# Where TensorE does the attention's small steps: head sums, a first exchange and the last scores moved into the midst of projections

## The chip, the cores and the metric

The kernel runs on one core of one Trainium2 chip. The metric is the device time of one execution in microseconds. Three runs of the kernel before gave 2029.91, 2032.22 and 2032.23 us, a median of 2032.22.

## The reference

A trunk of four layers over 256 tokens of width 1024, all in fp32. Each layer is a feed-forward block, a mixer and a feed-forward block:

```python
for i in range(DEPTH):                       # DEPTH = 4
    x = x + 0.5 * _swiglu(_rms_norm(x, norm_ffn1[i]), ...)
    h = _rms_norm(x, norm_mix[i])
    y = fox (i = 0, 3), conv module (i = 1), diff attention (i = 2)
    x = x + y
    x = x + 0.5 * _swiglu(_rms_norm(x, norm_ffn2[i]), ...)
```

The change touches the two kinds of attention. Fox has 16 heads of 64; q and k are RMS-normalised per head, and a cumulated forget gate is added to the scores before a causal softmax:

```python
q = _rms_norm(q, q_gain); k = _rms_norm(k, k_gain)
s = einsum(q, k) * scale + cum_q - cum_k     # cum: running sum of log_sigmoid(forget logits)
p = softmax(where(causal, s, -inf));  o = einsum(p, v);  y = o @ w_out
```

Diff attention has 8 heads of twice 64; q and k get a partial rotary embedding after the norm, and two softmaxes are combined:

```python
q = _partial_rope(_rms_norm(q, q_gain), cos, sin); k likewise
a = p[:, :, 0] - lam * p[:, :, 1];  o = _rms_norm(einsum(a, v), sub_gain) * (1 - lambda_init)
y = o @ w_out
```

## The kernel before

The activations stay transposed in SBUF, 8 tiles of 128 features by 256 tokens. Every weight is read once, in blocks of 1 MB: a DMA puts a block into one of five raw slots, ScalarE (ACT) rounds it to its high part (`split_high`, line 468), VectorE (DVE) subtracts to get the low part (`split_low`, line 774), and TensorE (PE) multiplies in three passes, high by high, low by high and high by low (lines 1332 to 1334). In the attention each such pass has 256 moving columns.

Each engine has its own program, an order written out by hand; an engine works strictly in that order and waits on semaphores that the others raise. There is no planner. So the place of a call in an engine's list decides what waits behind it.

An attention phase has four groups of 256 features (4 heads in fox, 2 double heads in diff). For group j PE does the projections of q (bank 0), k (bank 1) and v (bank 2), each block in two halves of 24 matmuls, and between them the small steps for group j and for the attention of group g = j - 1:

- `head_sums("q")`, `head_sums("k")` (line 1585): the squares of q or k, made by ACT (line 575), are summed over each head by a matmul with a matrix of ones. ACT takes Ln and Exp of the result (lines 567, 570, tiles q_inv, k_inv), and DVE multiplies (`normed`, line 992). In fox both sums go into bank 3, and k's waits until ACT has read q's (`q_log_ready`). k's products give kT, from which the scores of the next step are made.
- `swapped` (line 1590, diff): PE exchanges the rotated features by a permutation matrix; DVE multiplies by sines and cosines (lines 1001, 1007) and adds (line 1014).
- `score_pair(r)` (line 1531, in fox also 1539 for the gates): scores of two heads into banks 4 and 5. DVE masks and takes the maximum (lines 1025 or 1028, and 1032), ACT exponentiates (line 582), DVE normalises (line 1044) or combines (`combine`, lines 1055 and 1060).
- `turn(m)` (line 1552) transposes the probabilities, ACT copies them out (line 602, tile probsT), and `values(m)` (lines 1569, 1570) multiplies them with v. The second fox `score_pair` waits until the copies 0 and 1 are made, for it writes over their banks.

After the last group comes a tail: the attention of group 3 stands among the four blocks of the output projection, `o_block` (48 matmuls each, for o_part of groups 0 to 3). In diff, `o_sums` (line 1595) makes the norm of o.

The lists of ACT and DVE matter as much. In diff, for j of 2 and 3, ACT does in this order: o_squares, split_high(b+3j+2), inverse("o"), square("q"), o_part, exps(0), inverse("q"), exps(1), split_high(b+3j+3), copy_probs(0), square("k"), split_high(b+3j+4), exps(2), exps(3), inverse("k"), copy_probs(1). DVE does: split_low(b+3j+2), o_normalised, raw_part("q"), mask 0 and 1, o_part, normed("q"), combine(0), split_low(b+3j+3), rotary_cos("q"), raw_part("k"), mask 2, rotary_sin("q"), mask 3, rotary_sum("q"), split_low(b+3j+4), combine(1), normed("k"), and the rotary steps of k. In fox, for j of 1 to 3, ACT ends with exps(2), square("k"), inverse("q"), exps(3), split_high(b+3j+4), inverse("k"), copy_probs(2), copy_probs(3).

In fox's group 0 DVE also splits the cumulated gates (`split_cum`), and then GpSimd (POOL) spreads them over the heads in four instructions (`spread_cums`, line 424), while DVE goes on.

Of the kernel before, what the change touches and what calls it, by code (L numbers as in the profile page):

```python
# [18 lines left out]
KT = D // P  # L19
# [39 lines left out]
def build_trunk(nc, A, out):  # L59
# [12 lines left out]
    with ExitStack() as ctx:  # L72
# [106 lines left out]
        u = u_pad[:, :, TAPS - 1:TAPS - 1 + SEQ]  # L179
# [7 lines left out]
        bank = [banks[:, i, :] for i in range(8)]  # L187
# [271 lines left out]
        def _(act):  # L459
# [97 lines left out]
            def attention(i):  # L557
                a, b, fox = number(i), starts[i], phases[i] == "fox"
# [60 lines left out]
                def fox_group(j, u=0):  # L619

                    g = j - 1
                    split_high(b + 3 * j + 2)
                    if not j:
                        softplus()
                    square("q", j, u)
                    if j:
                        exps(0, g, u)
                        exps(1, g, u)
                    split_high(b + 3 * j + 3)
                    if j:  # L630
                        copy_probs(0, g, u)
                        copy_probs(1, g, u)
                        exps(2, g, u)
                    square("k", j, u)
                    inverse("q", j, u)
                    if j:
                        exps(3, g, u)
                    split_high(b + 3 * j + 4)
                    inverse("k", j, u)
                    if j:  # L640
                        copy_probs(2, g, u)
                        copy_probs(3, g, u)
                        o_part(g, u)
# [125 lines left out]
        def _(dve):  # L769
# [202 lines left out]
            def attention(i):  # L972
# [152 lines left out]
                def fox_group(j, u=0):  # L1125
                    g = j - 1
                    if not j:
                        logits()
                    split_low(b + 3 * j + 2)
                    if not j:  # L1130
                        cumulate()
                    raw_part("q", j, u)
                    if j:
                        mask_and_max(0, g, u)
                        mask_and_max(1, g, u)
                        normalise(0, g, u)
                        normalise(1, g, u)
                        split_low(b + 3 * j + 3)
                        mask_and_max(2, g, u)
                        raw_part("k", j, u)  # L1140
                        mask_and_max(3, g, u)
                    else:
                        raw_part("k", j, u)
                        split_low(b + 3 * j + 3)
                        split_cum()
                    normed("q", j, u)
                    if j:
                        normalise(2, g, u)
                        normalise(3, g, u)
                    split_low(b + 3 * j + 4)  # L1150
                    normed("k", j, u)
                    values(j, u)
                    if j:
                        o_part(g, u)
# [175 lines left out]
        def _(pe):  # L1330
# [178 lines left out]
            def attention(i):  # L1509
# [88 lines left out]
                def fox_group(j, u=0):  # L1598
                    g = j - 1
                    q_blk, k_blk, v_blk = (b + 3 * j + n for n in range(3))  # L1600
                    if j:
                        wait_block(q_blk)
                        columns_half(bank[0], q_blk, 0)
                        columns_half(bank[0], q_blk, 1).then_inc(S["block_done"], 1)
                        score_pair(0, g, u)
                    else:
                        first_block(i, bank[0])
                        forget_gates()
                    wait_block(k_blk)
                    columns_half(bank[1], k_blk, 0)  # L1610
                    columns_half(bank[1], k_blk, 1).then_inc(S["block_done"], 1)
                    if j:
                        turn(0, g, u)
                        turn(1, g, u)
                    else:
                        turn_cum()
                    head_sums("q", j, u)
                    wait_block(v_blk)
                    if j:
                        pe.wait_ge(S["v_ready"], 4 * a + j + u)  # L1620
                    tokens_half(bank[2], v_blk, 0, range(3))
                    if j:
                        score_pair(1, g, u)
                    tokens_half(bank[2], v_blk, 0, range(3, KT))
                    if j:
                        values(0, g, u)
                        values(1, g, u)
                    head_sums("k", j, u)
                    tokens_half(bank[2], v_blk, 1, range(6))
                    if j:  # L1630
                        turn(2, g, u)
                        turn(3, g, u)
                    tokens_half(bank[2], v_blk, 1, range(6, KT)).then_inc(S["block_done"], 1)
                    if j:
                        values(2, g, u)
                        values(3, g, u)

                def diff_group(j, u=0):
                    g = j - 1
                    q_blk, k_blk, v_blk = (b + 3 * j + n for n in range(3))  # L1640
                    if j:
                        wait_block(q_blk)
                        columns_half(bank[0], q_blk, 0)
                        if j > 1:
                            o_sums(g - 1, u)
                        columns_half(bank[0], q_blk, 1).then_inc(S["block_done"], 1)
                        score_pair(0, g, u)
                        head_sums("q", j, u)
                    else:
                        first_block(i, bank[0])  # L1650
                    wait_block(k_blk)
                    columns_half(bank[1], k_blk, 0)
                    columns_half(bank[1], k_blk, 1).then_inc(S["block_done"], 1)
                    if j:
                        turn(0, g, u)
                        score_pair(1, g, u)
                        swapped("q", j, u)
                    else:
                        head_sums("q", j, u)
                    wait_block(v_blk)  # L1660
                    if j:
                        pe.wait_ge(S["v_ready"], 4 * a + j + u)
                    tokens_half(bank[2], v_blk, 0)
                    if j:
                        values(0, g, u)
                    head_sums("k", j, u)
                    if not j:
                        swapped("q", j, u)
                    tokens_half(bank[2], v_blk, 1).then_inc(S["block_done"], 1)
                    if j:  # L1670
                        turn(1, g, u)
                    swapped("k", j, u)
                    if j:
                        values(1, g, u)

                def forget_gates():
# [23 lines left out]
                if fox:  # L1700
                    fox_group(0)
                    for j in range(1, GROUPS):
                        fox_group(j)
                    score_pair(0, g, 0)

                    pe.wait_ge(S["v_ready"], 4 * a + GROUPS)
                    o_block(0)
                    turn(0, g, 0)
                    turn(1, g, 0)
                    score_pair(1, g, 0)  # L1710
                    o_block(1)
                    values(0, g, 0)
                    values(1, g, 0)
                    turn(2, g, 0)
                    turn(3, g, 0)
                    o_block(2, (0, 4))
                    values(2, g, 0)
                    values(3, g, 0)
                    o_block(2, (4, KT))
                    o_block(3)  # L1720
                else:
                    for j in range(GROUPS):
                        diff_group(j)
                    score_pair(0, g, 0)
                    o_sums(g - 1, 0)

                    pe.wait_ge(S["v_ready"], 4 * a + GROUPS)
                    o_block(0)
                    turn(0, g, 0)
                    score_pair(1, g, 0)  # L1730
                    o_block(1, (0, 4))
                    values(0, g, 0)
                    o_block(1, (4, KT))
                    turn(1, g, 0)
                    o_block(2, (0, 1))
                    values(1, g, 0)
                    o_block(2, (1, 4))
                    o_sums(g, 0)
                    o_block(2, (4, KT))
                    o_block(3)  # L1740

            def conv(i):
# [82 lines left out]
```

## Time and profile before

| | |
|---|---|
| runs | 2029.91, 2032.22, 2032.23 us |
| profiled execution | 2030.45 us, span from first to last instruction 2028.7 us |
| mean granted TensorE clock | 0.999 |
| PE busy | 1984.2 us, 98% of the span |
| DVE busy, ACT busy | 1424.9 us (70%), 1046.1 us (52%) |
| first fox phase, diff phase, second fox phase | about 207 to 342, 1196 to 1334, 1702 to 1837 us |

The profile page gives such busy times, the chain that ended last and the costliest groups of instructions. The queries behind it give the instructions of a stretch in order of time, with the idle time of the engine ahead of each and what ended it, and sums of waits. A busy time of 98% is a share of the whole span; what the change can do is decided in the places where PE stands idle in the three attention phases.

### The profile page before, as it was taken

How to read it: one execution, taken by the hardware profiler on the slowest of the kernel's cores; microseconds unless marked ns; L12 is line 12 of the kernel's file. 1: busy time of each engine (PE TensorE's matmuls, PEld its weight loads, DVE VectorE, ACT ScalarE, POOL GpSimd, SP SyncE). 2: the span in 40 equal slices, each digit the busy share in tenths (PEclk: the TensorE clock that was granted, in tenths of full speed). 3: DMA queues.
4: the chain of work that ended last, by engine and by line, in shares of the span. 5: the costliest groups of instructions: out<-in, count | busy, mean ns of one | idle time of the engine just before them, and what ended most of it. 6: DMA issues, size and time to landing. Idle time of an engine off the chain costs nothing.

```text
span 2028.7 us, 29076 instructions
## 1 busy us (share of the span) xinstructions
PE 1984.2 (98%) x12584; PEld 1742.9 (86%) x12584; DVE 1424.9 (70%) x1631; ACT 1046.1 (52%) x1247; POOL 110.2 (5%) x120
## 2 busy tenths in 40 slices
PE   7999999999999998999999999999999999999999
PEld 6888888888888896988888888888888888888887
DVE  6876767876787554777587658887658765778763
ACT  5644456654555344654365455665446545456542
POOL 1000201000200001100000000010010001101000
PEclk9999999999999999999999999999999999999999
DMA  6655433655665583565656553355565555335653
GB/s 209 201 187 183 146 125 113 200 189 184 188 188 186 185 247 88 183 191 182 193 187 193 175 182 125 110 182 187 177 197 187 187 183 172 125 114 177 187 182 108
DMA packets 336365, 350.14 MB, mean 173 GB/s; under 512 B 10077, under 2 KB 331886, under 8 KB 336238
## 3 DMA queue, kind: packets, MB, share of 16 engines
q1 hardware_dynamic: 331742, 343.58, 53.3%
q10 hardware_dynamic: 4496, 4.70, 1.0%
q8 instruction: 99, 1.62, 0.3%
q14 instruction: 28, 0.23, 0.0%
HBM read 346.04 MB, written 2.22 MB: 172 GB/s over the span
## 4 chain that ended last, share of the span: by engine, by line
PE 89%; DVE 5%; ACT 4%; issue 1%; DMA 1%; ACTq 0%; SPq 0%; DVEq 0%
PE banks L1341 48%; PE banks L1346 25%; PE banks L1332 4%; PE banks L1333 4%; PE banks L1334 4%; ACT sb_w_high L468 1%; DVE sb_w_low L774 1%; ACT sb_scores L582 1%; PE banks L1531 1%; PE banks L1761 1%; PE banks L1569 1%; DMA sb_raw<-in_ffn_w_up 1%; DVE sb_neg_max L1032 0%; PE banks L1585 0%; PE banks L1552 0%
## 5 line engine op out<-in xcount | busy, mean ns | idle before, releaser
L774 DVE TENSOR_TENSOR sb_w_low<-sb_raw,sb_w_high 128x2048 fp32r<-128x2048 f32 (+1 forms) x332 | 752.4, 2271 | 241.3 <-ACT sb_w_high L468 240.9
L1341 PE MATMUL banks<-sb_x_both,sb_w_high 128*128 128x512 f32 x2816 | 727.0, 394 | 7.1 <-DVE sb_x_both L818 7.1
L468 ACT ACTIVATE sb_w_high<-sb_raw 128x2048 fp32r<-128x2048 f32 (+1 forms) x332 | 618.7, 1867 | 155.9 <-DMA sb_raw<-in_ffn_w_down 113.7
L1341 PEld LDWEIGHTS banks<-sb_x_both,sb_w_high 128*128 128x128 f32 x2816 | 500.9, 189 | 89.8 <-issue 7.5
L1346 PEld LDWEIGHTS banks<-sb_x_both,sb_w_low 128*128 128x128 f32 x2816 | 398.3, 190 | 36.0
L1346 PE MATMUL banks<-sb_x_both,sb_w_low 128*128 128x256 f32 x2816 | 408.1, 282 | 0.0
L1341 PE MATMUL banks<-sb_h_both,sb_w_high 128*128 128x512 f32 x1408 | 360.7, 395 | 0.0
L1341 PEld LDWEIGHTS banks<-sb_h_both,sb_w_high 128*128 128x128 f32 x1408 | 251.6, 188 | 46.7
L1346 PEld LDWEIGHTS banks<-sb_h_both,sb_w_low 128*128 128x128 f32 x1408 | 194.6, 188 | 17.1
L1346 PE MATMUL banks<-sb_h_both,sb_w_low 128*128 128x256 f32 x1408 | 200.3, 282 | 0.0
L1332 PE MATMUL banks<-sb_x_both,sb_w_high 128*128 128x256 f32 x512 | 148.7, 291 | 0.0
L486 ACT ACTIVATE sb_x_both<-sb_xT,sb_vec 128x256 fp32r<-128x256 f32 x96 | 43.6, 502 | 197.9 <-DVE sb_xT L807 176.7
L1333 PE MATMUL banks<-sb_x_both,sb_w_high 128*128 128x256 f32 x512 | 144.8, 283 | 0.0
L1334 PE MATMUL banks<-sb_x_both,sb_w_low 128*128 128x256 f32 x512 | 144.8, 283 | 0.0
L527 ACT ACTIVATE sb_up_part<-banks 128x512 f32<-128x512 f32 x88 | 52.4, 596 | 178.6 <-PE banks L1341 178.6
L527 ACT ACTIVATE sb_gate_part<-banks 128x512 f32<-128x512 f32 x88 | 52.4, 596 | 165.5 <-PE banks L1341 165.5
L931 DVE TENSOR_TENSOR sb_up_part<-banks,sb_up_part 128x512 f32<-128x512 f32 x88 | 60.7, 689 | 63.7 <-ACT sb_up_part L527 63.7
L1332 PEld LDWEIGHTS banks<-sb_x_both,sb_w_high 128*128 128x128 f32 x512 | 98.1, 192 | 3.2 <-issue 3.0
L1333 PEld LDWEIGHTS banks<-sb_x_both,sb_w_high 128*128 128x128 f32 x512 | 98.1, 192 | 1.6 <-issue 1.4
L915 DVE TENSOR_TENSOR sb_gate_part<-banks,sb_gate_part 128x512 f32<-128x512 f32 x88 | 60.7, 690 | 54.6 <-ACT sb_gate_part L527 54.4
L1334 PEld LDWEIGHTS banks<-sb_x_both,sb_w_low 128*128 128x128 f32 x512 | 98.1, 192 | 0.0
L804 DVE SCALAR_TENSOR_TENSOR sb_xT<-banks,sb_xT 128x512 f32<-128x512 f32 x32 | 22.1, 691 | 98.6 <-PE banks L1341 98.6
(210 smaller groups left out, 1950.8 us busy)
## 6 DMA issues: line engine op xcount, KB each, us to landing
sb_raw<-in_ffn_w_gate SPq DMA_DIRECT2D x88, 1024.0 KB, 5.4
sb_raw<-in_ffn_w_up SPq DMA_DIRECT2D x88, 1024.0 KB, 5.4
sb_raw<-in_ffn_w_down SPq DMA_DIRECT2D x64, 1024.0 KB, 5.0
sb_raw<-in_ffn_w_down SPq DMA_DIRECT2D x32, 768.0 KB, 4.3
sb_raw<-in_fox_w_in SPq DMA_DIRECT2D x24, 1024.0 KB, 5.2
sb_raw<-in_conv_w_pw SPq DMA_DIRECT2D x12, 1024.0 KB, 5.4
sb_raw<-in_diff_w_in SPq DMA_DIRECT2D x12, 1024.0 KB, 5.1
sb_raw<-in_fox_w_out SPq DMA_DIRECT2D x8, 1024.0 KB, 4.9
```

What stands on the lines that cost most here:

```text
L468: act.activation(slot(w_high, b)[:, 0:width(b)], slot(raw, b)[:, 0:width(b)], ACT.Copy).then_inc(S["high_ready"], 1)
L486: act.activation(x_high[:, t, :], xT[:, t, :], ACT.Copy, scale=vec[:, col + t:col + t + 1]).then_inc(S["xhigh_ready"], 1)
L527: act.activation((up_part if which else gate_part)[:, :, :], banks[:, at:at + 2, SEQ:], ACT.Copy).then_inc(S["up_part_ready" if which else ...
L774: dve.tensor_tensor(slot(w_low, b)[:, 0:width(b)], slot(raw, b)[:, 0:width(b)], slot(w_high, b)[:, 0:width(b)].bitcast(F32), ALU.subtract) ...
L804: dve.scalar_tensor_tensor(xT[:, 2 * T:2 * T + 2, :], sums[:, :, SEQ:], 0.5, xT[:, 2 * T:2 * T + 2, :], ALU.mult, ALU.add).then_inc(S["x_h ...
L915: dve.tensor_tensor(gate_part[:, :, :], banks[:, at:at + 2, 0:SEQ], gate_part[:, :, :], ALU.add).then_inc(S["gate_sum_ready"], 1)
L931: dve.tensor_tensor(up_part[:, :, :], banks[:, at:at + 2, 0:SEQ], up_part[:, :, :], ALU.add).then_inc(S["up_sum_ready"], 1)
L1332: pe.matmul(dst, s_high, m_high, start=first, stop=False, skip_group_check=loose)
L1333: pe.matmul(dst, s_high, m_low, start=False, stop=False, skip_group_check=loose)
L1334: return pe.matmul(dst, s_low, m_high, start=False, stop=last, skip_group_check=loose)
L1341: return pe.matmul(pair(bank[at][:, :]), high[:, n * P:(n + 1) * P], m_both, start=first, stop=last, skip_group_check=True)
L1346: pe.matmul(bank[at][:, SEQ:2 * SEQ], low[:, n * P:(n + 1) * P], m_high, start=False, stop=False, skip_group_check=True)
```

## The change

Only orders are changed; no instruction is added or removed, and every operand, semaphore and bank stays. Some calls are cut in two ranges. Fox:

- Group 0: ACT and DVE split block b+4 after inverse("k") and normed("k"), not ahead of them.
- Groups 1 to 3: PE's `head_sums("k")` comes after the first 3 of 8 tiles (9 matmuls) of v's second half, not ahead of them.
- Tail: 3 of 8 column tiles (18 matmuls) of `o_block(1)` come ahead of `score_pair(1)`.

Diff:

- Group 0's `swapped("k")` goes from the end of group 0 to the middle of group 1's q block.
- Groups 1 to 3: `head_sums("q")` goes from ahead of the k block to the middle of it (24 matmuls later).
- Tail: half of `o_block(0)` (24 matmuls) comes ahead of `score_pair(0)`, and `o_sums(3)` comes one column tile (6 matmuls) earlier within `o_block(2)`.

```diff
 # ACT, fox_group (DVE's fox_group likewise, with split_low and normed)
-                    split_high(b + 3 * j + 4)
+                    if j:
+                        split_high(b + 3 * j + 4)
                     inverse("k", j, u)
+                    if not j:
+                        split_high(b + 4)
 # PE, fox_group
-                    head_sums("k", j, u)
-                    tokens_half(bank[2], v_blk, 1, range(6))
+                    else:
+                        head_sums("k", j, u)
+                    tokens_half(bank[2], v_blk, 1, range(3))
+                    if j:
+                        head_sums("k", j, u)
+                    tokens_half(bank[2], v_blk, 1, range(3, 6))
 # PE, diff_group
                         if j > 1:
                             o_sums(g - 1, u)
+                        else:
+                            swapped("k", 0, u)
                         columns_half(bank[0], q_blk, 1).then_inc(S["block_done"], 1)
                         score_pair(0, g, u)
-                        head_sums("q", j, u)
...
                     columns_half(bank[1], k_blk, 0)
+                    if j:
+                        head_sums("q", j, u)
                     columns_half(bank[1], k_blk, 1).then_inc(S["block_done"], 1)
...
-                    swapped("k", j, u)
-                    if j:
+                    if j:
+                        swapped("k", j, u)
                         values(1, g, u)
 # PE, tail of fox
+                    o_block(1, (0, 3))
                     score_pair(1, g, 0)
-                    o_block(1)
+                    o_block(1, (3, KT))
 # PE, tail of diff
+                    o_block(0, (0, 4))
                     score_pair(0, g, 0)
                     o_sums(g - 1, 0)
-                    o_block(0)
+                    o_block(0, (4, KT))
...
-                    o_block(2, (1, 4))
+                    o_block(2, (1, 3))
                     o_sums(g, 0)
-                    o_block(2, (4, KT))
+                    o_block(2, (3, KT))
```

## Rows read from the trace of the kernel before

**Rows 1.** The page: PE's busy time, its share of the span, instructions.
```profile
PE 1984.2 (98%) x12584; PEld 1742.9 (86%) x12584; DVE 1424.9 (70%) x1631; ACT 1046.1 (52%) x1247; POOL 110.2 (5%) x120
```
**Rows 2.** Sums of PE's waits: total us, times, longest us.
```profile
PE banks L1585 <- ACT sb_q_inv L567: 4.8, 6, 0.8
```
**Rows 3.** PE in time order, third fox group: start, us, instruction, idle ahead.
```profile
279.94 1.10 PE L1585 MATMUL banks<-sb_k_square,sb_ones_heads 128*128 128x512 f32 x2 [0.80 <-ACT sb_q_inv L567]
...
284.80 0.81 PE L1569 MATMUL banks<-sb_probsT,sb_v_nat 128*64 128x256 f32 x3 [0.25 <-ACT sb_probsT L602]
```
**Rows 4.** ACT in time order, the same group.
```profile
277.71 0.40 ACT L582 ACTIVATE sb_scores<-sb_scores,sb_neg_max 128x128 f32<-128x128 f32 x1 [3.80 <-DVE sb_neg_max L1032]
...
281.24 1.90 ACT L468 ACTIVATE sb_w_high<-sb_raw 128x2048 fp32r<-128x2048 f32 x1
...
284.28 0.85 ACT L602 ACTIVATE sb_probsT<-banks 128x384 f32<-128x384 f32 x2
```
**Rows 5.** DVE in time order, fox, end of group 0.
```profile
231.44 3.98 DVE L774 TENSOR_TENSOR sb_w_low<-sb_raw,sb_w_high 128x2048 fp32r<-128x2048 f32 x1
235.34 2.38 DVE L992 SCALAR_TENSOR_TENSOR sb_kT<-sb_gate_scaled,sb_vec,sb_k_inv 128x512 f32<-128x512 f32 x1
...
238.43 3.19 DVE L774 TENSOR_TENSOR sb_w_low<-sb_raw,sb_w_high 128x2048 fp32r<-128x2048 f32 x1
```
**Rows 6.** POOL in time order, the same stretch (four instructions merged).
```profile
229.08 10.40 POOL L424 TENSOR_TENSOR sb_wide<-sb_cum_parts,sb_head_of_row 128x1024 bf16<-128x1024 bf16 x4 [17.18 <-DVE sb_cum_parts L1116]
```
**Rows 7.** PE in time order, fox group 1: first scores, second turn.
```profile
237.82 0.93 PE L1531 MATMUL banks<-sb_kT,sb_qT 64*128 64x128 f32 x8 [0.92 <-issue]
...
246.41 0.55 PE L1552 MATMUL banks<-sb_ident,sb_scores 128*128 128x128 f32 x3 [0.60 <-DVE sb_scores L1044]
```
**Rows 8.** PE in time order, fox tail: second scores, third and fourth turn.
```profile
321.09 0.93 PE L1531 MATMUL banks<-sb_kT,sb_qT 64*128 64x128 f32 x8 [0.72 <-ACT sb_probsT L602]
...
328.94 0.88 PE L1552 MATMUL banks<-sb_ident,sb_scores 128*128 128x128 f32 x6
```
**Rows 9.** DVE in time order, fox tail: the last normalisation.
```profile
326.01 0.55 DVE L1044 TENSOR_SCALAR sb_scores<-sb_scores,sb_inv_sum 128x128 f32<-128x128 f32 x2
```
**Rows 10.** PE in time order, diff: exchange of group 0, q's head sum of group 1.
```profile
1218.52 1.13 PE L1590 MATMUL banks<-sb_gate_scaled,sb_swap 128*128 128x512 f32 x2 [1.31 <-DVE sb_gate_scaled L992]
...
1227.09 1.13 PE L1585 MATMUL banks<-sb_q_square,sb_ones_heads 128*128 128x512 f32 x2 [0.85 <-ACT sb_q_square L575]
```
**Rows 11.** PE in time order, diff group 2, and group 3's first scores.
```profile
1251.72 0.28 PE L1333 MATMUL banks<-sb_x_both,sb_w_high 128*128 128x256 f32 x1
1251.84 0.28 PE L1334 MATMUL banks<-sb_x_both,sb_w_low 128*128 128x256 f32 x1
1252.05 0.93 PE L1531 MATMUL banks<-sb_kT,sb_qT 64*128 64x128 f32 x8
1253.57 1.12 PE L1585 MATMUL banks<-sb_q_square,sb_ones_heads 128*128 128x512 f32 x2 [0.59 <-ACT sb_q_square L575]
...
1278.78 0.93 PE L1531 MATMUL banks<-sb_kT,sb_qT 64*128 64x128 f32 x8
```
**Rows 12.** ACT in time order, diff group 2: Ln of q's head sums.
```profile
1255.08 0.67 ACT L567 ACTIVATE sb_q_inv<-banks,sb_eps 128x512 f32<-128x512 f32 x1
```
**Rows 13.** DVE in time order, diff group 2.
```profile
1259.13 2.29 DVE L774 TENSOR_TENSOR sb_w_low<-sb_raw,sb_w_high 128x2048 fp32r<-128x2048 f32 x1 [0.20 <-ACT sb_w_high L468]
...
1269.68 0.74 DVE L992 SCALAR_TENSOR_TENSOR sb_gate_scaled<-sb_gate_scaled,sb_vec,sb_k_inv 128x512 f32<-128x512 f32 x1
```
**Rows 14.** PE in time order, diff tail: first scores, first turn.
```profile
1300.01 0.93 PE L1531 MATMUL banks<-sb_kT,sb_qT 64*128 64x128 f32 x8 [1.02 <-DVE sb_kT L1014]
...
1308.22 0.55 PE L1552 MATMUL banks<-sb_ident,sb_scores 128*128 128x128 f32 x3 [0.48 <-DVE sb_scores L1060]
```
**Rows 15.** Stretches at the conv phase's idle: length; PE, PEld, DVE, ACT, POOL busy; PEclk; DMA.
```profile
795.40:800.40 5.00, 0.00 (x0) 0.00 (x0) 4.42 (x6) 3.69 (x6) 0.00 (x0) 1.00 0.00 0
800.40:803.80 3.40, 2.83 (x13) 2.83 (x14) 1.49 (x3) 3.34 (x7) 0.00 (x0) 0.51 0.00 0
```

More of the change, by code:

```diff
@@ L1149, in fox_group @@
                         normalise(3, g, u)
-                    split_low(b + 3 * j + 4)
+                    if j:
+                        split_low(b + 3 * j + 4)
                     normed("k", j, u)
+                    if not j:
+                        split_low(b + 4)
                     values(j, u)
```

## Prediction

> **What bounds the kernel now.** The page comes first: PE is busy 98% of the span [rows 1], so anything gained must come from the places where it idles. The sums of waits name them: the largest that this change aims at is PE at a head sum, waiting for ACT's reading of bank 3, six times 0.8 us [rows 2]. But a wait tells only where PE stands, not what sets the time. So I read next PE, ACT and DVE in time order through one group of each phase, and asked of each wait: if PE didn't wait here, would it wait at its next meeting with the same chain? The reader is to see in rows 3 and 4, and in 11 to 13, that ACT and DVE run without a gap from one meeting with PE to the next. There PE's idle time is only slack of a loop whose length the other two engines set. Single projection matmuls start 0.12 us apart [rows 11]; 24 of them take 2.9 us, a full block 5.8.
>
> **Fox, groups 1 to 3: 0.** The head sum of k waits 0.80 [rows 3]. Put 9 matmuls (1.1 us) later it needs no wait, so PE is some 0.7 us early at turn(2). The next meeting is values(2), which already waits 0.25 for ACT's copies [rows 3]. ACT's list there is exps(2) at 277.71 (after 3.80 of idling for the mask, that is for PE's second scores), squares, both halves of q's inverse, exps(3), split_high at 281.24, k's inverse, copies at 284.28, with no gap from 277.71 on [rows 4]. k's inverse runs behind split_high (281.24 + 1.90 = 283.1); the head sum, now at about 280.3, is done by 281.4. So the copies come when they did, values(2) starts at 284.80 as before, and its wait grows from 0.25 to about 1. Six waits of 0.8 go and six of 0.7 to 0.8 come. What would be lost without that cover is nothing either: one more switch between kinds of matmul costs PE about 0.1, inside the new wait.
>
> **Fox, group 0: +0.1 a phase.** PE waits 0.92 for the first scores [rows 7], for kT is made at 235.34, behind split_low(b+4), which starts at 231.44 [rows 5]. With the order turned, DVE makes kT first. But DVE is slow here because POOL works: kT takes 2.38 where the same line takes 0.74 in diff, and w_low 3.98 and 3.19 where it takes 2.29 there [rows 5, 13], while POOL's four instructions stretch over 10.40 us [rows 6]. Taking turns, with POOL first: kT runs 231.44 to 233.9, w_low of b+4 233.8 to 237.9, v 237.8 to 238.6, w_low of b+5 238.6 to 241.8, where it ended at 241.62 before. So the scores start at 236.9, 0.9 early; block b+4 is ready at 237.9, just when PE comes (236.9 + 1.1). The next meeting is turn(1), which waits 0.60 for DVE's normalisation [rows 7], and DVE does that behind the second w_low and the masks, without a gap. It moves by +0.1. Bounds: 0 if the order costs DVE nothing, +1.9 if DVE loses one turn more to POOL (10.40 / 4 = 2.6 with waiting, less 0.7 of waiting); I take the row nearest, the unchanged total.
> The Trainium skill, "SBUF — State Buffer", section "SBUF: two separate sides", says that VectorE and GpSimd take a shared pair of ports by an exclusive lock for a whole instruction. The trace agrees (2.38 against 0.74), and by that rule the turns come out as above; were it bandwidth that is shared, kT would end a little earlier, with the same sum.
>
> **Fox, tail: -0.8 a phase.** The second scores wait 0.72 for both copies [rows 8]. Now 18 matmuls (2.2 us, and 0.1 for a switch) stand there, and the scores start at 322.4, not 321.09: +1.35. Everything behind them on DVE and ACT is 1.35 later: the last normalisation ends at 326.01 + 0.55 + 1.35 = 327.9. PE, with the wait gone, reaches turn(2) at 328.94 - 0.8 = 328.1 [rows 8, 9]. It just fits, 0.2 to spare and 0.3 more for turn(3). The copies and the last o_low have over 1 us of cover (24 more matmuls of o_block(2)). Bounds: -0.4 if turn(3) waits, -0.8. I take -0.8.
>
> **Diff, group 1: +0.35.** `swapped("k")` of group 0 waits 1.31 [rows 10]. In the middle of the q block it doesn't: q's first half begins at 1217.1, the exchange stands at 1220.0, DVE reads it at 1221.3 as before, and the first scores start at 1223.85 and not at 1227.09 - 0.85 - 0.93 = 1225.3: 1.45 early. But the head sum of q now comes 24 matmuls behind them: 1223.85 + 0.93 + 2.9 = 1227.7, against 1227.09. ACT read it 3.03 after the first scores before (as in rows 11 and 12: 1255.08 - 1252.05), at 1228.35; now ACT can have it 1.05 behind its start (its record, whose end is modelled, is 1.12 long [rows 11]), at 1228.7. So q's inverse comes 0.35 later, and with it all below.
>
> **Diff, groups 2 and 3: +1.85 each. This is the step that decides.** Before, the head sum of q waits 0.59 for ACT's squares (1253.57, which is 1.52 behind the scores at 1252.05) [rows 11]; ACT takes its Ln at 1255.08, straight behind exps(0) [rows 12]. After, PE does 24 matmuls first: 1252.05 + 0.93 + 2.9 = 1255.9 for the head sum, and 1.05 more for ACT, 1256.95. Waiting in ACT's queue behind q's inverse are exps(1) and split_high(b+3j+3); DVE's normed("q"), combine(0) and split_low(b+3j+3) wait for those (the last by 0.20 at 1259.13) [rows 13], and DVE then has no idle moment until k's norm at 1269.68 [rows 13]. PE starts the next group's first scores 9.10 behind that (1278.78) [rows 11], by its own work and one more exchange. So the loop is: scores to k's norm 17.63, set by ACT and DVE; k's norm to scores 9.10, set by PE; together 26.73. The first part grows by 1256.95 - 1255.08 = 1.85 (1.8 to 1.95). PE's own work in that part has fewer waits than before and isn't the limit: the first turn waits about 1.2, the second about 1.4. Bounds: -0.7 a group (PE's wait of 0.59 and its switch saved, if PE's list alone set the time), +1.85. The value next to the rows is the upper, for they show no gap.
>
> **Diff, tail: +1.7.** The first scores wait 1.02 for kT; 24 matmuls ahead of them take 2.9 with a switch: +1.8 net. Scores to first turn is 8.21, at whose end PE already waits 0.48 for DVE's combine [rows 14]; this part isn't shortened, and now only 24 matmuls lie in it, so PE idles some 3.4 us there. The earlier o_sums(3) finds its squares not quite ready and gains 0.1.
>
> **Sum.** Fox 2 x (0 + 0.13 - 0.8) = -1.3; diff 0.35 + 2 x 1.85 + 1.7 = +5.75; together +4.4 us. DMA has no part: no attention split waits for a landing, and the loads, released by block_done, move by under 2 us at most. On the profiled execution (2030.45) that makes 2034.9; it lies 1.8 under the median of the three runs, whose two upper ones agree within 0.01. I give 2036.2, near the median plus 4.4 (2036.6), a bit toward the profiled one.
>
> **Rivals.**
> 1. *The waits simply go.* Head sums 6 x 0.8; first scores of fox 2 x 0.92; second scores of the tails 2 x 0.72; diff 1.31, 0.85, 2 x 0.59, 1.02: 12.4 us, less 0.8 for the switches: 2020.6. For it: each of these waits is truly there. Against it: values(2) and the turns wait already.
> 2. *Diff's chain has slack after all; the kernel is not slower.* If q's norm isn't what split_low(b+3j+3) hangs on, groups 2 and 3 are PE's: -0.7 each, group 1 -1.45, tail +1.7, fox -1.3: -2.4, so 2029.8. It decides at ACT's Ln of q: it must not come later than exps(0) ends. For it: PE's wait at the second turn is under 0.2. Against it: 24 matmuls are 2.9 us, the slack there 0.5.
> 3. *The clock falls in the new idle time of diff's tail.* After the conv phase's idle of 5 us the granted clock was 0.51 (1.2 and not 2.4 GHz) for 3.4 us, in which PE made 13 matmuls in 2.83 us, 0.1 us more for each: 1.3 us [rows 15]. In the tail it would add up to that: 2037.5. Against it: 3.4 us is shorter than 5. The Trainium skill, "TensorE: Matmul & The Clock Gate", section "HAM oscillation — how this bites in real kernels", warns of such gaps; by that rule the time would be this 2037.5; the trace agrees for the idle of 5 us [rows 15].
> 4. *DVE loses a turn to POOL in fox's group 0.* +1.9 in each fox phase: 2039.8. Block b+4 would come late, and turn(1) too.
>
> **Chances.** Forecast 0.67, rival 1 0.05, rival 2 0.13, rival 3 0.08, rival 4 0.07. Range: 2031.5 to 2039.0; it leaves out rival 1, half of rival 4 and most of rival 2. Two medians of this kernel are told apart at about 0.2%, that is 4.1 us, and the forecast lies hard by it: of its chance I put 0.4 to slower and 0.27 to the same; rivals 3 and 4 are nearly all slower (0.13), rival 1 faster (0.05); of rival 2 0.03 is faster and 0.10 the same. Faster 0.08, same 0.39, slower 0.53.
>
> **What would show it.** Right: in groups 2 and 3 of diff first scores to first scores takes 28.6 and not 26.7, ACT waits for PE at q's Ln, and PE waits over 1 us at both turns; in fox the wait of the k head sum is gone, values(2) waits about 1 us, and the group still takes 26.4; diff's tail has an idle of about 3.4 at the first turn; fox's tail is 0.8 shorter. Wrong: a diff group of 26 us, or a fox group under 26. In that case the chain that I call closed has a gap which I didn't see.

## The result: 0.4% slower, more than forecast

The changed kernel took 2040.48 us, the median of five runs (2036.3 to 2042.7), and the kernel before 2032.22 beside it. The ratio is 1.0042 (95% interval 1.0031 to 1.0052), +8.3 us where the forecast's sum had +4.4. The forecast was 2036.2 and its range ended at 2039.0, so the time lies above it. The same kernel measured again on another occasion gave 2037.74 beside 2031.02, a ratio of 1.0033 (1.002 to 1.0046); that is inside the range, but not for the forecast's reasons, as is shown below.

The profiled execution took 2042.7 us, with a span of 2040.9, 12.2 us longer than that of before. Page, busy times (answers to [rows 1]):

```profile
PE 1991.9 (98%) x12584; PEld 1747.8 (86%) x12584; DVE 1424.0 (70%) x1631; ACT 1046.0 (51%) x1247; POOL 110.1 (5%) x120
```

PE has the same 12584 matmuls and is 7.7 us longer busy: part of the loss is inside the matmuls and not in waits. The sums of PE's waits, as in [rows 2] (total us, times, longest), first before, then changed:

```profile
PE banks L1552 <- DVE sb_scores L1044: 1.9, 4, 0.6
...
PE banks L1569 <- ACT sb_probsT L602: 1.5, 6, 0.3
...
PE banks L1552 <- DVE sb_scores L1060: 0.5, 1, 0.5
```
```profile
PE banks L1558 <- DVE sb_scores L1063: 10.1, 7, 3.4
...
PE banks L1575 <- ACT sb_probsT L602: 5.5, 6, 0.9
PE banks L1558 <- DVE sb_scores L1047: 3.8, 4, 1.3
```

The head sums of k no longer wait: the 4.8 us of [rows 2] are gone. In their place `values` waits for ACT's copies 5.5 us where it waited 1.5, the turns of diff wait for DVE's combine 10.1 where it was 0.5, and those of fox for its normalisation 3.8 where it was 1.9. Nearly every wait went to PE's next meeting with the same chain; only the 0.72 ahead of the second scores in each fox tail [rows 8] did not come back.

PE in diff, in time order (start, us, instruction, idle ahead), answers to [rows 11, 14]: first scores of groups 1 to 3 and of the tail, head sums of q, turns of group 2, and the tail's first turn.

```profile
1226.82 0.93 PE L1537 MATMUL banks<-sb_kT,sb_qT 64*128 64x128 f32 x8
...
1255.41 0.93 PE L1537 MATMUL banks<-sb_kT,sb_qT 64*128 64x128 f32 x8
1259.24 1.02 PE L1591 MATMUL banks<-sb_q_square,sb_ones_heads 128*128 128x512 f32 x2
...
1264.22 0.55 PE L1558 MATMUL banks<-sb_ident,sb_scores 128*128 128x128 f32 x3 [1.10 <-DVE sb_scores L1063]
...
1275.06 0.55 PE L1558 MATMUL banks<-sb_ident,sb_scores 128*128 128x128 f32 x3 [1.12 <-DVE sb_scores L1063]
...
1284.01 0.93 PE L1537 MATMUL banks<-sb_kT,sb_qT 64*128 64x128 f32 x8
...
1308.89 0.93 PE L1537 MATMUL banks<-sb_kT,sb_qT 64*128 64x128 f32 x8
...
1317.13 0.90 PE L1558 MATMUL banks<-sb_ident,sb_scores 128*128 128x128 f32 x3 [3.39 <-DVE sb_scores L1063]
```

First scores to first scores: 28.59 and 28.60 us, where [rows 11] have 26.73. ACT in group 2 (as [rows 12]) and DVE's norm of k (as [rows 13]):

```profile
1260.30 0.69 ACT L567 ACTIVATE sb_q_inv<-banks,sb_eps 128x512 f32<-128x512 f32 x1 [1.76 <-PE banks L1591]
```
```profile
1274.92 0.75 DVE L995 SCALAR_TENSOR_TENSOR sb_gate_scaled<-sb_gate_scaled,sb_vec,sb_k_inv 128x512 f32<-128x512 f32 x1
```

ACT, which had no gap there, now waits 1.76 for PE's head sum. It takes q's Ln 4.89 behind the scores, 1.86 later than before. Scores to k's norm is 19.51 (17.63 before), and k's norm to the next scores 9.09 (9.10 before).

Granted clock by stretches of the same execution (length; PE, PEld, DVE, ACT, POOL busy with counts; PEclk; DMA share; GB/s):

```profile
1310.00:1316.20 6.20, 3.74 (x26) 3.06 (x25) 4.19 (x15) 5.14 (x12) 0.00 (x0) 1.00 0.19 49
1316.20:1323.03 6.83, 5.90 (x27) 4.92 (x28) 5.50 (x14) 2.94 (x11) 0.00 (x0) 0.50 0.32 111
1323.03:1330.00 6.97, 6.97 (x57) 6.79 (x56) 3.73 (x7) 3.54 (x3) 0.00 (x0) 1.00 0.12 24
776.90:780.30 3.40, 3.40 (x40) 2.16 (x36) 3.40 (x3) 3.38 (x5) 0.00 (x0) 0.50 0.19 40
800.80:807.60 6.80, 4.11 (x19) 4.11 (x20) 4.00 (x7) 6.51 (x12) 0.00 (x0) 0.50 0.01 2
1753.10:1756.50 3.40, 3.40 (x15) 2.62 (x15) 2.29 (x1) 0.93 (x3) 0.00 (x0) 0.51 0.39 139
```

In the midst of the new idle time of diff's tail the clock went to its lower level (PEclk 0.50, that is 1.2 GHz), and came back at 1323.0. Its 27 matmuls would take about half of their 5.90 us at the full clock (an estimate). The next two stretches stand in the conv phase, which the change doesn't touch, and the last in group 1 of the second fox phase.

Where the time went, by the starts of the same matmuls before and after, in us against the kernel before:

| stretch | orders, forecast | this profile | second profile of the same kernel |
|---|---|---|---|
| before the first fox phase | 0 | +0.15 | -0.43 |
| first fox phase | -0.67 | -0.81 | +0.75, with one stretch at half clock |
| conv phase | 0 | +3.73 | -1.27 |
| diff phase | +5.75 | +8.41, with one stretch at half clock | +5.80, none |
| second fox phase | -0.67 | +0.72, with one stretch at half clock | -0.79, none |
| whole span | +4.4 | +12.2 | +4.1 |

### The profile page after: what moved, and what is told of

It reads as the page before. It is cut to its first block, busy times and chain, and to the rows that moved or that the text cites. A ratio compares the mean times of both kernels' runs of the same rounds, so it can differ in the third digit from the quotient of the medians.

```text
span 2040.9 us, 29079 instructions
## 1 busy us (share of the span) xinstructions
PE 1991.9 (98%) x12584; PEld 1747.8 (86%) x12584; DVE 1424.0 (70%) x1631; ACT 1046.0 (51%) x1247; POOL 110.1 (5%) x120
## 4 chain that ended last, share of the span: by engine, by line
PE 90%; DVE 4%; ACT 4%; issue 1%; DMA 1%; ACTq 0%; SPq 0%; DVEq 0%
PE banks L1347 48%; PE banks L1352 25%; PE banks L1338 4%; PE banks L1339 4%; PE banks L1340 4%; ACT sb_w_high L468 1%; DVE sb_w_low L777 1%; ACT sb_scores L582 1%; PE banks L1537 1%; PE banks L1776 1%; DMA sb_raw<-in_ffn_w_up 0%; PE banks L1591 0%; PE banks L1575 0%; DVE sb_neg_max L1035 0%; DMA u_away<-sb_u_pad 0%
```

## The experiments

Theory O: what counts is how late the chain of ACT and DVE is fed, so each part has the price that the forecast gave it by orders alone. Theory C: beside it the gathered idle times let the clock fall, and that is the rest. Rival W: the waits that were removed are worth what they show. The kernel before had a median of 2031.02 beside the first four kernels of the table, 2031.17 beside the next four and 2031.12 beside the last four; differences below are between medians.

| kernel | what it has of the change | median, us (runs) | ratio, 95% |
|---|---|---|---|
| fox_parts | all of fox | 2029.98 (11) | 0.9998 (0.9989 to 1.0006) |
| diff_groups | diff's groups | 2034.74 (11) | 1.0020 (1.0011 to 1.0029) |
| diff_tail | diff's tail | 2034.74 (11) | 1.0021 (1.0012 to 1.0030) |
| after_again | all | 2037.74 (5) | 1.0033 (1.0020 to 1.0046) |
| diff_tail_filled | diff's tail, idle time filled | 2032.91 (11) | 1.0010 (1.0001 to 1.0019) |
| good_parts | fox groups 1 to 3 and tail, `swapped("k")`, `o_sums(3)` | 2029.91 (11) | 0.9996 (0.9987 to 1.0005) |
| fox_split_early | below | 2022.74 (5) | 0.9957 (0.9945 to 0.9969) |
| both_improved | below | 2020.58 (5) | 0.9944 (0.9932 to 0.9957) |
| f0_alone | order in fox's group 0 | 2031.78 (11) | 1.0005 (0.9996 to 1.0013) |
| q_sum_6 | head sum of q after 6 matmuls | 2031.51 (11) | 1.0002 (0.9993 to 1.0011) |
| q_sum_24 | head sum of q after 24 | 2037.14 (7) | 1.0032 (1.0020 to 1.0043) |
| after_tail_back | all but the tail's scores | 2034.01 (11) | 1.0016 (1.0007 to 1.0025) |

**The parts: fox_parts, diff_groups, diff_tail, after_again.** The first three have one phase's part of the diff each, the fourth is the changed kernel itself.

> Only the fox parts of the change (order of the splits in group 0, the later head sum of k, 18 matmuls ahead of the second scores in the tail). Theory 'orders and clock': the orders give -0.8 us in each fox tail and +0.1 in each group 0, -1.3 together, but the waits of PE in fox's group 1, which now stand together at the first and second turn (1.4 + 0.6 us), let the clock fall in some runs, about +1.4 each time: 2031 to 2033. In the profile a fox group takes 26.4 us as before and values(2) waits about 1 us. Rival 'the orders alone': no loss by the clock, -1.3 in every run: 2031. Rival 'the waits simply go': -8 us, 2024.

> Only two parts: swapped('k') of diff's group 0 in the middle of group 1's q block, and the head sum of q in the middle of the k block. Theory 'orders and clock': +0.3 in group 1, +1.85 in each of groups 2 and 3, +4.0 together, and the tail as before: 2036.2 if the clock stays up. First scores to first scores 28.6 us. Rival 'the change's loss of 8 us is all order, the diff groups are mis-sized': +6 or more here, with a longer group than 28.6.

> Only the two parts in diff's tail: half of o_block(0) ahead of the first scores, o_sums(3) one column tile earlier. Theory 'orders and clock': +1.7 by the order (first scores to first turn stays 8.2 us, PE idles 3.7 us in it), and after that idle the clock falls to half for 3.4 or 6.8 us, which costs 1.3 to 2.7 more: 2035 to 2036.6. Rival 'the orders alone': the fall of the clock in the changed kernel was chance, here it stays up: 2033.9.

> The changed kernel once more, for its clock and for the conv phase. Theory 'orders and clock': +4.3 us by the orders, the rest by stretches at half clock: each profile shows the same intervals between PE's steps where the clock is up, and the low stretches differ in number from one run to the next; 2036 to 2043. If the conv phase's loss of 3.7 us in the first profile is chance, it is gone here or seen in the other kernels too; if it belongs to the change, it is here again and in none of the three others.

diff_groups: the diff phase +4.05 in its profile, no half clock in it; the forecast's 0.35 + 2 x 1.85 exactly. diff_tail: the diff phase +3.29, of which the order is 1.8 (the phase is +1.77 in the filled kernel below) and the rest the clock. fox_parts: each phase gives back its 0.8 and then loses 1.55 at half clock, where 0.7 of gain stood in the orders. So in these profiles O holds for the sizes of the orders in every part, and C for what is beside them. The medians of the three parts, -1.0, +3.7 and +3.7, add up to +6.4, beside +6.7 for the whole. fox_parts can't be told from the kernel before, and it came out 1.0 us under the range that was expected for it: its profile, with a fall of the clock in both phases, is one of its slower runs. diff_groups came out 1.5 under its 2036.2, which was counted from the first occasion's median for the kernel before. Fox in the profile of fox_parts, group 1: PE in time order, and two stretches by clock.

```profile
244.72 0.55 PE L1558 MATMUL banks<-sb_ident,sb_scores 128*128 128x128 f32 x3 [1.32 <-DVE sb_scores L1047]
245.86 0.55 PE L1558 MATMUL banks<-sb_ident,sb_scores 128*128 128x128 f32 x3 [0.60 <-DVE sb_scores L1047]
246.24 1.72 PE L1591 MATMUL banks<-sb_q_square,sb_ones_heads 128*128 128x512 f32 x2
```
```profile
243.50:246.40 2.90, 1.08 (x7) 0.85 (x8) 1.84 (x8) 2.72 (x7) 0.00 (x0) 1.00 0.59 164
246.40:249.80 3.40, 3.40 (x12) 2.21 (x10) 2.29 (x1) 1.18 (x3) 0.00 (x0) 0.51 0.48 168
```

Before, the waits of this place lay apart: 0.92 at the first scores, 0.60 at the second turn [rows 7], and at the first turn this one:

```profile
245.27 0.55 PE L1552 MATMUL banks<-sb_ident,sb_scores 128*128 128x128 f32 x3 [0.35 <-DVE sb_scores L1044]
```

With kT made earlier the 0.92 is gone, and its time stands at the first turn (1.32, not 0.35), close to the 0.60. Behind those two the clock is at 1.2 GHz, and the head sum takes 1.72 instead of 1.02.

**The idle time in diff's tail: diff_tail_filled.** It is diff_tail with 24 matmuls on a free bank, whose results nobody reads:

```diff
                     o_block(0, (4, KT))
+                    for _ in range(24):
+                        pe.matmul(bank[7][:, 0:SEQ], x_high[:, 0, 0:P], x_high[:, 0, :], start=True, stop=True)
                     turn(0, g, 0)
```

> The kernel of diff_tail with 24 more matmuls (2.9 us, of activations that are at hand, into bank 7, whose old content has been read and which values(0) overwrites later) ahead of the first turn, where PE idles 3.7 us. Theory 'the clock falls through the idle': the matmuls cost nothing, since they lie in the idle; the order's +1.7 stays (first scores to first turn 8.2 us), but no stretch at half clock follows, so +1.7 over the kernel before instead of diff_tail's +3.7. Rival 'the half clock has nothing to do with this idle': it is seen behind the tail here too, and the time is diff_tail's.

PE at scores and first turn and the stretches by clock, first diff_tail, then filled:

```profile
1303.11 0.93 PE L1531 MATMUL banks<-sb_kT,sb_qT 64*128 64x128 f32 x8
...
1311.35 0.55 PE L1552 MATMUL banks<-sb_ident,sb_scores 128*128 128x128 f32 x3 [3.39 <-DVE sb_scores L1060]
1311.82 1.45 PE L1531 MATMUL banks<-sb_kT,sb_qT 64*128 64x128 f32 x8
```
```profile
1312.10:1315.50 3.40, 3.40 (x19) 2.75 (x17) 3.40 (x9) 1.24 (x5) 0.00 (x0) 0.50 0.13 44
```
```profile
1302.86 0.93 PE L1531 MATMUL banks<-sb_kT,sb_qT 64*128 64x128 f32 x8
...
1307.54 3.04 PE L1731 MATMUL banks<-sb_x_both 128*128 128x256 f32 x24
1311.10 0.55 PE L1552 MATMUL banks<-sb_ident,sb_scores 128*128 128x128 f32 x3 [0.51 <-DVE sb_scores L1060]
1311.57 0.93 PE L1531 MATMUL banks<-sb_kT,sb_qT 64*128 64x128 f32 x8
```
```profile
1312.10:1315.50 3.40, 3.40 (x29) 3.07 (x26) 3.39 (x10) 1.18 (x6) 0.00 (x0) 1.00 0.05 16
```

Scores to first turn is 8.24 in both, so the chain takes what it took and the extra matmuls cost nothing. But behind the turn the same 3.40 us hold 29 records instead of 19, and the second scores take 0.93 instead of 1.45. The median falls from +3.7 to +1.7, which is the order's own price. The two were run on different occasions and the intervals of their ratios just overlap (1.0012 to 1.0030 and 1.0001 to 1.0019), but 10 of diff_tail's 11 runs took 2034.0 or more, and 9 of the filled kernel's 11 took 2033.6 or less. So filling the idle time took the fall away: that the idle time let the clock fall is shown as far as one profile of each and the medians can show it. W is out here: with useless work in place of the wait the kernel is faster.

**How late may q's head sum be: q_sum_6, q_sum_24.** Both are the kernel before with only this call moved within the k block.

```diff
                         score_pair(0, g, u)
-                        head_sums("q", j, u)
...
-                    columns_half(bank[1], k_blk, 0)
+                    columns_half(bank[1], k_blk, 0, range(2))     # q_sum_6; q_sum_24: the whole half
+                    if j:
+                        head_sums("q", j, u)
+                    columns_half(bank[1], k_blk, 0, range(2, KT))
```

> Only q's head sum of diff's groups 1 to 3, put 6 matmuls (0.7 us) into the k block instead of ahead of it. Theory 'a closed chain of ACT and DVE': PE's wait of 0.59 us there goes, ACT's Ln of q comes when it did (behind exps(0), 0.5 us later than it could), and the time is that of the kernel before within 0.5 us; the saved wait comes back at the turns. Rival 'PE's waits are the time': -0.6 in each of three groups, -1.8.

> Only q's head sum of diff's groups 1 to 3, put 24 matmuls (2.9 us) into the k block as in the change; the exchange of group 0 stays where it was. Theory 'a closed chain': +1.85 in each of three groups, for group 1's first scores no longer come 1.5 us early: +5.5 by the order, 2036.7. If the exchange in the q block had no part in it, it would be +4.0 as in diff_groups.

ACT's Ln of q in group 2, first with 6 matmuls ahead, then with 24:

```profile
1255.34 0.67 ACT L567 ACTIVATE sb_q_inv<-banks,sb_eps 128x512 f32<-128x512 f32 x1
```
```profile
1259.88 0.69 ACT L567 ACTIVATE sb_q_inv<-banks,sb_eps 128x512 f32<-128x512 f32 x1 [1.76 <-PE banks L1585]
```

With 6 the wait of 0.59 [rows 11] is gone, ACT's Ln still comes straight behind its exponentials, and the kernel is as fast as before (+0.4, unclear against 0). A group takes 26.72. Of PE's 2.0 us of waits at these head sums 1.4 stand again at the turns. With 24 ACT waits 1.76, a group takes 28.61, and the kernel loses 6.0 us, three times 1.85 and a little (5.6 in the diff phase of its profile). The wait was worth nothing, the lateness all.

**The clock falls behind other gathered waits, and one order costs nothing: good_parts, f0_alone, after_tail_back.** They are made of parts of the diff alone; the last is the changed kernel with the first scores of diff's tail where they were.

> The change without its three parts that I hold to be harmful: left out are the order of the splits in fox's group 0, q's head sum in the midst of the k block, and o_block(0) ahead of the first scores. Theory: -0.8 in each fox tail, 0 from the later head sum of k, 0 or +0.1 from the exchange in the q block (S to k's norm is then ACT's and DVE's), -0.1 from o_sums(3): -1.6, with no stretch at half clock in any attention phase: 2029.4. If the fall of the clock in fox's group 1 has nothing to do with where PE's waits stand, it is seen here as well, at about 246 or 1741 us.

> Only the order of the splits in fox's group 0 (block b+4 behind k's norm). Theory 'waits gathered in one place let the clock fall': by the order +0.1 in each fox phase; PE's waits of 0.92, 0.35 and 0.60 us become one of 1.4 and one of 0.6 us within 3 us, and in one or both fox phases of the profile the clock falls there to half for 3.4 us, at about 246 or 1741 us, +1.5 each time: 2031.3 to 2034.3. Rival 'the fall comes from the later head sum of k': no fall here, +0.2.

> The changed kernel with diff's o_block(0) put back behind the first scores. Theory 'orders and clock': the changed kernel's +4.3 by orders less 1.8, and less the fall of the clock behind the tail (about 2): +2.5 by orders and +0.8 to 1.5 by the clock in fox's group 1: 2033.5 to 2035. Rival: if the tail's part were only its order, 2035.5 or more.

good_parts was to gain 1.6 us. Its median is 1.3 under the kernel before, and its interval has 1 in it. Its 11 runs lie in two groups: seven at 2029.3 to 2030.1 with mean granted clocks of 0.996 and 0.997, and four at 2031.6 to 2032.8 with 0.995. The profile is one of the four: each fox phase is 0.8 shorter, but diff is 1.33 longer, and it shows why. PE in diff's group 1, and the stretch behind:

```profile
1228.92 2.08 PE L1585 MATMUL banks<-sb_q_square,sb_ones_heads 128*128 128x512 f32 x2 [2.43 <-ACT sb_q_square L575]
```
```profile
1228.90:1232.30 3.40, 3.38 (x10) 2.35 (x11) 1.40 (x6) 2.22 (x7) 0.00 (x0) 0.50 0.33 112
```

The waits for the exchange (1.31) and for the head sum (0.85) [rows 10] have become one of 2.43, and the clock fell behind it. f0_alone: the two fox phases are as long as before (to 0.02), with the gathered waits of 1.33 and 0.60 in place. The fall that was expected in one or both is not there: in this execution the clock held. after_tail_back lies 2.9 above before, where the orders alone make 2.4 in its profile (diff +3.99, each fox phase -0.81, no half clock in any of the three); the changed kernel lay 6.7 above.

**Shorten the chain instead: fox_split_early, both_improved.** In fox ACT idles 3.80 ahead of exps(2) and has then no gap to copy_probs(2) [rows 4], and in that stretch stands a split of 1.90 that is not due yet. So it goes into the idle time:

```diff
                         copy_probs(1, g, u)
+                        split_high(b + 3 * j + 4)
                         exps(2, g, u)
                     square("k", j, u)
...
                         exps(3, g, u)
-                    split_high(b + 3 * j + 4)
+                    else:
+                        split_high(b + 4)
                     inverse("k", j, u)
```

It also has the parts of fox's groups 1 to 3, fox's tail and `o_sums(3)`. both_improved adds `swapped("k")` in group 1, q's head sum after 6 matmuls, and in diff's groups 0 to 2 the split of block b+3j+4 behind k's inverse (ACT) and behind `rotary_cos("k")` (DVE).

> Fox: the later head sum of k and the tail's 18 matmuls as in the change, and ACT does split_high(b+3j+4) ahead of exps(2), where it idles 3.8 us for the mask, instead of between exps(3) and k's inverse; diff: only o_sums(3) earlier. Theory 'values(2) is set by ACT's list': k's inverse and the copies come 1.9 us earlier on ACT, so the saved wait of the head sum now reaches values(2): -1.0 in each of six fox groups, and kT is earlier in the tail: with the two tails -0.8 each, -7.5 together: 2023.5. Rival 'the waits are PE's own or another chain holds values(2)': -1.6 as with the tails alone.

> As fox_split_early, and in diff: the exchange of group 0 in the q block of group 1; q's head sum after 6 matmuls of the k block (0.7 us, within the 0.5 to 0.6 us by which ACT's exps(0) is later anyway); and in groups 0 to 2 the split of block b+3j+4 on ACT and DVE behind k's inverse and k's rotary_cos, out of the chain from the first scores to k's norm. Theory: this chain gets 1 us shorter in groups 1 and 2, then PE's own list sets it: 25.7 us from first scores to first scores, -2 together and 0 to -1 more from group 1's first scores: 2020.5 to 2021.5. Rival: the chain has another member as late as the one removed, and diff takes what it did: 2023.5.

ACT and PE of fox_split_early in the third fox group (as [rows 3, 4]):

```profile
272.12 1.92 ACT L468 ACTIVATE sb_w_high<-sb_raw 128x2048 fp32r<-128x2048 f32 x1
276.04 0.40 ACT L582 ACTIVATE sb_scores<-sb_scores,sb_neg_max 128x128 f32<-128x128 f32 x1 [2.00 <-DVE sb_neg_max L1034]
...
281.02 1.01 ACT L602 ACTIVATE sb_probsT<-banks 128x384 f32<-128x384 f32 x2
```
```profile
278.57 1.02 PE L1587 MATMUL banks<-sb_k_square,sb_ones_heads 128*128 128x512 f32 x2
...
282.14 0.66 PE L1571 MATMUL banks<-sb_probsT,sb_v_nat 128*64 128x256 f32 x4
```

From exps(2) to the copies ACT takes 4.98 where it took 6.57; values(2) doesn't wait. Each fox phase is 4.2 shorter, where PE's orders without the earlier split had given 0.8, all of it in the tail. The kernel is 8.4 faster. The earlier split without PE's orders was not run, so the gain belongs to the two together. In both_improved diff's group 2 takes 25.57 from first scores to first scores and not 26.73, and the phase is 2.16 shorter. At 2020.58 it is the fastest of all, 10.6 us under before.

## Why the prediction was wrong

**Right, by its own steps.** Fox groups 1 to 3: the head sum waits no more, values(2) waits 0.92, nothing is gained. PE in the changed kernel (as [rows 3]):

```profile
280.38 1.02 PE L1591 MATMUL banks<-sb_k_square,sb_ones_heads 128*128 128x512 f32 x2
...
284.95 0.81 PE L1575 MATMUL banks<-sb_probsT,sb_v_nat 128*64 128x256 f32 x3 [0.92 <-ACT sb_probsT L602]
```

The group's values(2) is 0.15 later than before, which is the offset from the start. Fox group 0, DVE (as [rows 5]):

```profile
231.59 2.38 DVE L995 SCALAR_TENSOR_TENSOR sb_kT<-sb_gate_scaled,sb_vec,sb_k_inv 128x512 f32<-128x512 f32 x1
233.89 3.98 DVE L777 TENSOR_TENSOR sb_w_low<-sb_raw,sb_w_high 128x2048 fp32r<-128x2048 f32 x1
...
238.58 3.19 DVE L777 TENSOR_TENSOR sb_w_low<-sb_raw,sb_w_high 128x2048 fp32r<-128x2048 f32 x1
```

That is the forecast's list to 0.2 us; rival 4 (a turn lost to POOL) is out. The +0.13 for this order isn't seen: f0_alone's fox phases are as long as before. Fox's tail gave 0.8. There the forecast's own terms (2.2 + 0.1 - 0.72) make 1.6 and not the 1.35 that it states for the second scores; they came 1.36 later. Diff's group 1: scores 1.57 earlier (1.45 forecast), then +0.3; groups 2 and 3 +1.87 each; the tail +1.8. Rivals 1 and 2 are out: waits of 4.8 us went and nothing came of it. The sum by orders, +4.4, is right to 0.2: the execution of the changed kernel in which the diff phase kept its clock shows +5.80 there for 5.75, and a fox phase at full clock -0.8 for -0.67, together +4.2.

**The step that failed.** The sum has no term for the clock: the forecast put its cost at nothing, with the reason that the new idle of 3.4 us is shorter than the 5 us behind which the clock had fallen. The runs show 2.0 us in its place for diff's tail alone (diff_tail against diff_tail_filled), and about 2.5 for the changed kernel on the second occasion (+6.7 against +4.2 by orders). On the first occasion the gap was 4.1, and a part of it stays open, as said below.

**Wrong in detail: rival 3.** The clock stood there as a rival, with a chance of 0.08, one place, and 1.3 us. Three things failed in it.

- The reason against it, "3.4 us is shorter than 5", took the only fall in the trace of before for the least that causes one. The idle time came as forecast (3.39), and behind it the clock fell in two of the three profiles of kernels with that order and unfilled idle (changed kernel, diff_tail; not after_again).
- The places: it fell also in group 1 of fox, in 4 of the 10 fox phases profiled with the new order of group 0 (changed kernel one, fox_parts two, after_again one; f0_alone and after_tail_back none), and in none of the 18 in profiles without it. The forecast had priced that order by when work is done and not by where PE's waits then stand: 0.92 and, 7.5 us later, 0.35 and 0.60 became 1.33 and 0.60 within 2 us.
- The price: 1.3 to 1.6 where it stayed low for 3.4 us, with PE busy in all of it (2.83 of 3.40 in [rows 15]), and 2.6 for 6.8 us, not 1.3.

An estimate of the mean from these: the tail 2/3 x 2.1, fox 2 x 0.4 x 1.55, together +2.6; with the 4.2 of the orders +6.8. The changed kernel was measured at +8.3 and +6.7. The estimate rests on few profiles: by the medians the falls in fox are worth 0.5 to 0.7 (fox_parts, f0_alone and after_tail_back against their orders) and not 1.2, and the one in the tail 2.0 and not 1.4. The Trainium skill, "TensorE: Matmul & The Clock Gate", section "HAM oscillation — how this bites in real kernels", tells of a kernel in which the wait behind each burst of matmuls throws the clock back every time; here it was so in some executions and not in others.

**Chance.** Of the profile's +12.2, 3.7 lie in the conv phase, which no edit touches; there the second profile has -1.3. In the first, one of PE's waits for ACT there is 2.64 and not 1.15, and the clock is low for 10.2 us in all, against 3.4 in the second and before; behind that wait 256 matmuls take 15.71 and not 14.02. Why is not known. It may be one reason why the changed kernel's five runs spread over 6.4 us; the fastest of them (2036.3) had the highest mean granted clock, 0.997, and the second slowest (2041.31) the lowest, 0.993. How far the chances of a fall in the clock differ from one occasion to the next stays open: a profile shows one execution.

## What to carry to other kernels

Before removing a wait, ask whether PE's next meeting with the same chain waits too: if so, the wait only moves, and what gives something is to shorten the chain (here one split of 1.9 us moved into ACT's idle time made -8.4 us together with fox's orders, which by themselves gave about 1). What is put ahead of an instruction that feeds such a chain has to fit into that engine's slack: 6 matmuls did, 24 cost 1.85 us in each group. And when waits are gathered, also where the sum of idle time is the same, count the clock as a risk with its own price, or fill the gap with idle work.

## What the runs showed of the hardware

- The clock fell behind PE waits of 1.32 and 0.60 close together (4 of 10 phases), behind one of 2.43 (the one profile that has it), and in or behind one of 3.39 (2 of 3). It is no sure thing: f0_alone has the first and after_again the last, and the clock held there.
- Where PE has enough to do, a stretch of 3.4 us at half clock costs 1.3 to 1.6 us and one of 6.8 us, idle for a part, 2.6.
- Useless matmuls in a wait cost nothing measurable: 24 of them, 3.04 us, in an idle time of 3.39, left the turn 8.24 behind the scores.
- The order of VectorE's work beside POOL's four instructions changed no duration: 2.38, 3.98 and 3.19 us before and after.
- A head sum between projection matmuls costs PE no switch: it starts 0.12 us behind the last of them, as they do among themselves. First scores start 0.21 behind [rows 11], and so does `values`. The forecast's 0.1 for a switch holds for these and not for the head sum.
